# HGRN2 heads: the factor 1 - lb moves from the keys to the queries, both gates' sigmoids come first, and ScalarE copies the last level's score blocks

## Chip, core and metric

One NeuronCore of a Trainium2 chip runs the whole kernel. The metric is the device time of one execution in microseconds (us). The kernel before takes 2995.98 us (median of 3 runs, 2995.09 to 2998.92).

## The reference, cut to what matters

The network has two trunk layers: an HGRN2 gated linear recurrence in both directions, then a short convolution mixer, each followed by a dense SwiGLU FFN. All is float32. The change touches the recurrence alone. There are 8 heads of 128 channels, 1024 latent and 256 context tokens. For each head and direction:

```python
f = lb + (1.0 - lb) * jax.nn.sigmoid(zf)
log_f = jnp.log(jnp.maximum(f, F_FLOOR))
k = (1.0 - lb) * jax.nn.sigmoid(-zf)
...
o_inter = jnp.einsum("bhtk,bhkv->bhtv", qc * jnp.exp(cum), s)
scores = jnp.einsum("bhtk,bhsk,bhtsk->bhts", qc, kc, decay)
o = o_inter + jnp.einsum("bhts,bhsv->bhtv", scores, vc)
```

Every term of `o` holds q times k once, so the factor 1 - lb (one number for each channel) may stand on either.

## The kernel before

Each large product is three matmuls (high times high, high times low, low times high) of float32r halves. TensorE (PE) computes the projections of head h + 1 (five panels of 1024 x 128: both gates z_f and z_b, then q, v, g) and, between their pieces, the scan of head h. The first head (projections only) and the last (scan only) stand outside a loop of three passes with two heads each. All of it is written out by hand: each engine has its own program, and semaphores alone order them. On PE, `slots(n)` sets n pieces of three 512-column matmuls of the next head (or, behind a panel, a context block) between the steps of the scan.

The steps of one scan:

- ScalarE (ACT) computes the sigmoids of z_f and z_b into `gates` and of -z into `k`. VectorE (DVE) makes f of the gates, multiplies `k` by 1 - lb (L1726), applies the floor, then sums the keys of both directions (`k_sum`) and multiplies q by the gates into `q_all` (L1659).
- `diagonal`: PE multiplies q by k_sum for the diagonal of the scores (L782), and DVE takes it out of PSUM (`scores`, L1494).
- Seven levels, i = 0 to 6, each in two parts of four chunks. ACT merges the key halves into `k_both` (`merge_keys`), PE multiplies (`level`, L795), and DVE multiplies the keys (L1676) and queries (L1683) of both directions by the decay of their block, then copies the scores under a mask from PSUM (`copy_predicated`, L1685). After part 1 it multiplies the block totals (L1690).
- `key_transposes` and `key_values` (PE, L767 and L809), with ACT copying `k_tok` between them and DVE doing the states, forward first; then the outputs and their norm.

PSUM banks 4 and 5 take the scan's uses in turn, use 0, 2, ... and 1, 3, .... `scan_readers` names whose semaphore says that the bank's last use has been read. The forward key transposes come right behind level 6 in the same banks, and wait for the last totals_f too. ACT copies the next head's projections out of PSUM between its merges: z_f, z_b, then q (with the constant scale 128^-0.5) ahead of level 5 and between both parts of level 6. GpSimd (POOL) splits each weight panel into high and low parts (L522, L525).

Of the kernel before, what the change touches and what calls it, by code (L numbers as in the profile page):

```python
# [10 lines left out]
ALU = mybir.AluOpType  # L11
# [50 lines left out]
SCORE_EVACS = 16  # L62
# [54 lines left out]
def scan_readers(use):  # L117
    if use < U_DIAG:
        return [("scan_evac", ACT_EVACS, use)]
    if use < U_KF:  # L120
        return [("scores_evac", SCORE_EVACS, use - U_DIAG)]
    if use < U_KVF:
        return [("scan_evac", ACT_EVACS, 3 + use - U_KF)]
    if use < U_KB:
        return [("state_f", STATE_OPS, STATE_AT[use - U_KVF] - 1)]
    if use < U_KVB:
        return [("scan_evac", ACT_EVACS, 6 + use - U_KB)]
    if use < U_O:
# [23 lines left out]
def build_trunk(nc, x, ctx, cond, ada, ada_bias, norm_w, lb_raw, gnorm, conv_w,  # L152
# [105 lines left out]
    one_minus_lb = small("one_minus_lb", KB)  # L258
    gn = small("gn", 1)
# [19 lines left out]
    with ctx_mgr:  # L279
# [10 lines left out]
            sigmoids gates_done diag_ready scan_f scan_b k_merged scan_full scan_evac scores_evac state_f state_b  # L290
            gate_sig gs_ready o_squared o_gated o_sum_full ovar_done orstd_ready mix_ready mods_ready
# [6 lines left out]
        credit = {n: c for n, c in (("scan_evac", ACT_EVACS), ("scores_evac", SCORE_EVACS),  # L298
# [309 lines left out]
        def _(pe):  # L608
# [204 lines left out]
            def outputs(hh, part):  # L813

                pe.wait_ge(S["scores_evac"], hh * SCORE_EVACS + 2 * SCORE_EVACS)
                for d in (FWD, BWD):
                    pe.wait_ge(state_sem[d], hh * STATE_OPS + 2 * STATE_OPS)
                b = scan_use(hh, U_O + part)
                for c in range(4 * part, 4 * part + 4):
                    dst = bank(b, (c % 4) * P, (c % 4 + 1) * P)  # L820
                    pe.matmul(dst, v_tok[:, CCH + c, :], scores[:, c, :], start=True, stop=False)
                    pe.matmul(dst, state[FWD][:, c, :], chunk(qd[FWD], c), start=False, stop=False)
                    mm = pe.matmul(dst, state[BWD][:, c, :], chunk(qd[BWD], c), start=False, stop=True)
                mm.then_inc(S["scan_full"], 1)
# [294 lines left out]
        def _(act):  # L1119
# [46 lines left out]
            for name in ("scan_evac", "o_squared"):  # L1166
                act.sem_inc(S[name], credit[name])
# [50 lines left out]
            def head(gemm_of, scan_of, parity):  # L1218
# [26 lines left out]
                if hs is not None:  # L1245
# [5 lines left out]
                    act.wait_ge(S["scan_full"], hs * SCAN_USES + SCAN_USES)  # L1251
                    for d in (FWD, BWD):
                        copy(gates[d][:, :], z[d][:, :], "sigmoids", ACT.Sigmoid)
                        copy(k[d][:, :], z[d][:, :], "sigmoids", ACT.Sigmoid, scale=-1.0)
# [13 lines left out]
                def merge_keys(i, part):  # L1268

                    if i == 0:  # L1270

                        act.wait_ge(S["gates_done"], hs * 6 + 7)
# [38 lines left out]
                if hg is not None:  # L1311
# [4 lines left out]
                    evacuate(2, 0, cols(q, 0), scale=float(P) ** -0.5)  # L1316
# [3 lines left out]
                if hg is not None:  # L1320
                    evacuate(2, 1, cols(q, 1), scale=float(P) ** -0.5)
                if hs is not None:
                    merge_keys(6, 1)
                if hs is not None:
                    for part in range(3):
                        key_tokens(FWD, part)

                    for part in range(3):
                        key_tokens(BWD, part)
# [160 lines left out]
        def _(dve):  # L1490
# [27 lines left out]
            dve.wait_ge(S["params"], 7)  # L1518

# [130 lines left out]
            def head(gemm_of, scan_of):  # L1650
# [10 lines left out]
                def decay_level(i):  # L1661
# [3 lines left out]
                    for part in range(2):  # L1665
# [4 lines left out]
                        for d in (FWD, BWD):  # L1670
# [7 lines left out]
                            if d == BWD:  # L1678

                                dve.wait_ge(S["scores_evac"], hs * SCORE_EVACS + (SCORE_EVACS + 2 * i + part + 1))  # L1680
# [4 lines left out]
                        V.copy_predicated(scores[:, 4 * part:4 * part + 4, :],  # L1685
                                          masks[:, i, :].unsqueeze(1).broadcast_to([P, 4, P]),
                                          bank(use).rearrange("p (c t) -> p c t", t=P)
                                          ).then_inc(S["scores_evac"], 1)
                    for d in (FWD, BWD):
                        V.tensor_tensor(total_of(d, i + 1), tot[d][:, :, 0], tot[d][:, :, 1], ALU.mult  # L1690
                                        ).then_inc(scan_sem[d], 1)

# [24 lines left out]
                if hs is not None:  # L1717
                    lbs, oml = lb[:, bass.ds(hs, 1)], one_minus_lb[:, bass.ds(hs, 1)]
                    base_g = hs * 6 + 1
# [51 lines left out]
                elif hg is not None:  # L1771
                    for a in range(ADA_GROUP):
# [206 lines left out]
```

## Time and profile before

| | us |
|---|---|
| median of 3 runs | 2995.98 |
| the profiled execution, its own time | 2991.44 |
| its span | 2989.4 |
| PE busy | 2810.2 (94%) |
| DVE busy | 1446.8 (48%) |
| ACT busy | 721.7 (24%) |
| POOL busy | 761.7 (25%) |

An engine that is idle costs nothing unless the chain of work that ends last runs through it. The seven scans that share PE with projections lie between 130 and 892 us of the span, the scan of the last head between 892 and 1000 us. Granted clock is TensorE's, 1.00 for 2.4 GHz and 0.50 for 1.2 GHz. In rows of a timeline the first number is the start, the second the time to the end of the group, both in us, and the bracket tells how long the engine stood idle before, and what released it.

### The profile page before, as it was taken

To read this page: it belongs to the slowest core of one execution; us is meant where nothing else is said; L and a number is where in the kernel's file an instruction comes from. 1 tells how busy PE (TensorE), PEld (TensorE's weight loads), DVE (VectorE), ACT (ScalarE), POOL (GpSimd) and SP (SyncE) were. 2 spreads that over 40 slices of the span, in tenths; PEclk is the share of its full clock that TensorE was granted. 3 is DMA by queue.
4 is the path that set the end of the run, shared out by engine and by line. 5 is a ranking of instruction groups with operands and counts; after the bars stand their busy time and mean duration, and the time that the engine had idled before them with its cause. 6 is when DMAs were issued, how large, how long until landed. Compare 5 with 4: busy or idle time off the path is not lost.

```text
span 2989.4 us, 36417 instructions
## 1 busy us (share of the span) xinstructions
PE 2810.2 (94%) x13776; PEld 2358.3 (79%) x13776; DVE 1446.8 (48%) x2083; ACT 721.7 (24%) x1251; POOL 761.7 (25%) x361
## 2 busy tenths in 40 slices
PE   7989999999986899999999998999899999999997
PEld 5778778777875688888888887888688888888886
DVE  6377576577658232343242346556732323332236
ACT  5223223223323251111111116111143111111112
POOL 3322121212114311222222231344702222222222
PEclk9999999999997999999999999999999999999999
DMA  5111111111110201121111110332201111111111
GB/s 227 64 36 49 45 41 52 36 57 36 36 36 28 99 15 51 49 78 63 63 62 58 63 64 22 127 112 98 91 15 36 49 44 48 49 49 49 49 49 71
DMA packets 48742, 176.89 MB, mean 59 GB/s; under 512 B 5872, under 2 KB 5872, under 8 KB 48624
## 3 DMA queue, kind: packets, MB, share of 16 engines
q1 hardware_dynamic: 48624, 175.24, 17.2%
q8 instruction: 83, 1.36, 0.2%
q14 instruction: 35, 0.29, 0.0%
HBM read 171.02 MB, written 4.19 MB: 59 GB/s over the span
## 4 chain that ended last, share of the span: by engine, by line
PE 80%; DVE 12%; ACT 3%; issue 2%; DMA 1%; SPq 0%; POOL 0%; DVEq 0%; ACTq 0%; POOLq 0%
PE psum L613 18%; PE psum L615 17%; PE psum L614 17%; PE psum L1011 4%; PE psum L1012 4%; PE psum L1013 4%; PE psum L795 3%; DVE q_all L1683 2%; DVE k_all L1676 2%; PE psum L659 2%; PE psum L845 2%; PE psum L846 2%; PE psum L847 2%; DVE h_lo L1494 1%; DVE scores L1685 1%
## 5 line engine op out<-in xcount | busy, mean ns | idle before, releaser
L613 PE MATMUL psum<-h_hi,w_hi 128*128 128x512 f32 x2336 | 938.0, 402 | 8.0 <-POOL w_lo L525 4.9
L615 PE MATMUL psum<-h_hi,w_lo 128*128 128x512 f32 x2336 | 913.3, 391 | 0.0
L614 PE MATMUL psum<-h_lo,w_hi 128*128 128x512 f32 x2336 | 912.6, 391 | 0.0
L568 POOL TENSOR_TENSOR w_lo<-w_raw,w_hi 128x1024 fp32r<-128x1024 f32 x116 | 280.0, 2414 | 1032.6 <-ACT w_hi L1121 1032.6
L615 PEld LDWEIGHTS psum<-h_hi,w_lo 128*128 128x128 f32 x2336 | 440.1, 188 | 94.1
L613 PEld LDWEIGHTS psum<-h_hi,w_hi 128*128 128x128 f32 x2336 | 441.3, 189 | 90.7 <-POOL w_lo L525 5.3
L614 PEld LDWEIGHTS psum<-h_lo,w_hi 128*128 128x128 f32 x2336 | 441.6, 189 | 81.0
L522 POOL TENSOR_TENSOR w_hi<-w_raw,zero 128x1024 fp32r<-128x1024 f32 x74 | 151.7, 2050 | 1041.9 <-PE psum L613 926.8
L1494 DVE TENSOR_TENSOR hidden<-gate_act,up_copy 128x512 f32<-128x512 f32 x88 | 75.8, 861 | 655.3 <-ACT up_copy L1121 655.3
L1494 DVE TENSOR_TENSOR y<-y,psum 128x512 f32<-128x512 f32 x288 | 194.8, 686 | 202.4 <-PE psum L1013 199.9
L1011 PE MATMUL psum<-w_hi,hidden_hi 128*128 128x512 f32 x640 | 250.0, 391 | 0.3 <-DVE y L1494 0.3
L1013 PE MATMUL psum<-w_hi,hidden_lo 128*128 128x512 f32 x640 | 249.5, 390 | 0.0
L1012 PE MATMUL psum<-w_lo,hidden_hi 128*128 128x512 f32 x640 | 249.5, 390 | 0.0
L1121 ACT ACTIVATE w_hi<-w_raw 128x1024 fp32r<-128x1024 f32 x116 | 122.4, 1055 | 351.0 <-PE psum L613 178.9
L795 PE MATMUL psum<-q_all,k_both 128*128 128x128 f32 x896 | 138.8, 302 | 59.5 <-ACT k_both L1121 18.0
L795 PEld LDWEIGHTS psum<-q_all,k_both 128*128 128x128 f32 x896 | 127.5, 204 | 83.3 <-issue 24.4
L525 POOL TENSOR_TENSOR w_lo<-w_raw,w_hi 128x1024 fp32r<-128x1024 f32 x74 | 191.0, 2581 | 5.8
L1641 DVE SCALAR_TENSOR_TENSOR ada_acc<-ada_raw,silu_cond,ada_acc 128x512 f32<-128x512 f32 x140 | 158.8, 1134 | 51.5 <-DMA ada_raw<-in_ada 47.2
L1121 ACT ACTIVATE gate_act<-psum 128x512 f32<-128x512 f32 x88 | 52.6, 598 | 380.1 <-PE psum L615 380.1
L1121 ACT ACTIVATE up_copy<-psum 128x512 f32<-128x512 f32 x88 | 52.6, 598 | 377.9 <-PE psum L615 377.9
L1011 PEld LDWEIGHTS psum<-w_hi,hidden_hi 128*128 128x128 f32 x640 | 120.3, 188 | 25.6 <-DVE y L1494 0.9
L1013 PEld LDWEIGHTS psum<-w_hi,hidden_lo 128*128 128x128 f32 x640 | 120.4, 188 | 25.2
(216 smaller groups left out, 3537.0 us busy)
## 6 DMA issues: line engine op xcount, KB each, us to landing
w_raw<-in_w_ffn_in SPq DMA_DIRECT2D x88, 512.0 KB, 3.5
ada_raw<-in_ada SPq DMA_DIRECT2D x80, 512.0 KB, 4.4
w_raw<-in_w_ffn_out SPq DMA_DIRECT2D x44, 512.0 KB, 3.5
w_raw<-in_w_hgrn_in SPq DMA_DIRECT2D x40, 512.0 KB, 5.9
w_raw<-in_w_conv_in SPq DMA_DIRECT2D x24, 512.0 KB, 4.9
ada_first<-in_ada SPq DMA_DIRECT2D x4, 2048.0 KB, 15.5
x_start<-in_x SPq DMA_DIRECT2D x4, 1024.0 KB, 18.7
w_raw<-in_w_hgrn_out SPq DMA_DIRECT2D x8, 512.0 KB, 3.6
```

The costliest lines, as they stand in the source:

```text
L525: pool.tensor_tensor(lo[:, :], w_raw[:, slot, :], hi[:, :], ALU.subtract).then_inc(S["panel_split"], 1)
L568: pool.tensor_tensor(lo[:, :], w_raw[:, slot, :], hi[:, :], ALU.subtract).then_inc(S["panel_split"], 1)
L613: begin = pe.matmul(out_ap, hi[:, a:b], rhs_hi, start=first, stop=False)
L614: pe.matmul(out_ap, hi[:, a:b], rhs_lo, start=False, stop=False)
L615: return begin, pe.matmul(out_ap, lo[:, a:b], rhs_hi, start=False, stop=last)
L795: mm = pe.matmul(bank(b, (c % 4) * P, (c % 4 + 1) * P), chunk(k_both, c), both(q_all, c * P, 1 << i), start=True, stop=True)
L1011: begin = pe.matmul(dst, hidden_hi[buf][:, kb, tokens], hi[:, cols], start=first, stop=False)
L1012: pe.matmul(dst, hidden_hi[buf][:, kb, tokens], lo[:, cols], start=False, stop=False)
L1013: return begin, pe.matmul(dst, hidden_lo[buf][:, kb, tokens], hi[:, cols], start=False, stop=last)
L1121: nc.scalar.activation(dst, src, func, **kw).then_inc(S[sem], 1)
L1494: V.tensor_tensor(dst, a, b, op).then_inc(S[sem], 1)
L1641: V.scalar_tensor_tensor(ada_acc[:, :], src, weight, ada_acc[:, :], ALU.mult, ALU.add).then_inc(S["ada_step"], 1)
```

## The change

The keys are no longer multiplied: a copy of `one_minus_lb` times 128^-0.5 is made once (`q_scale`), DVE copies the next head's column of it to `head_scale`, and ACT takes that as the scale operand when it copies q out of PSUM. ACT does the sigmoids in the order gates_f, gates_b, k_f, k_b. At level 6 the mask holds just one 64 x 64 block for each direction and chunk, and ACT copies these blocks in place of DVE's masked copy of all 512 columns.

```diff
-SCORE_EVACS = 16
+SCORE_EVACS = 14
+
+LAST = LEVELS - 1
...
+    if use < U_LEVEL + 2 * LAST:
+        return [("scores_evac", SCORE_EVACS, use - U_DIAG)]
     if use < U_KF:
-        return [("scores_evac", SCORE_EVACS, use - U_DIAG)]
+        return [("last_scores", 4, 2 * (use - U_LEVEL - 2 * LAST) + 1)]
...
                 pe.wait_ge(S["scores_evac"], hh * SCORE_EVACS + 2 * SCORE_EVACS)
+                pe.wait_ge(S["last_scores"], hh * 4 + (credit["last_scores"] + 4))
...
                     for d in (FWD, BWD):
                         copy(gates[d][:, :], z[d][:, :], "sigmoids", ACT.Sigmoid)
+                    for d in (FWD, BWD):
                         copy(k[d][:, :], z[d][:, :], "sigmoids", ACT.Sigmoid, scale=-1.0)
...
-                    evacuate(2, 0, cols(q, 0), scale=float(P) ** -0.5)
+                    act.wait_ge(S["head_scaled"], hg + 1)
+                    evacuate(2, 0, cols(q, 0), scale=head_scale[:, 0:1])
...
-                    evacuate(2, 1, cols(q, 1), scale=float(P) ** -0.5)
+                    evacuate(2, 1, cols(q, 1), scale=head_scale[:, 0:1])
                 if hs is not None:
                     merge_keys(6, 1)
                 if hs is not None:
+                    b = 1 << LAST
+                    for part in range(2):
+                        src = bank(scan_bank(U_LEVEL + 2 * LAST + part)).rearrange("p (c t) -> p c t", t=P)
+                        for d in (FWD, BWD):
+                            rows, cs = slice(K_HALF[d] * b, K_HALF[d] * b + b), slice(Q_HALF[d] * b, Q_HALF[d] * b + b)
+                            copy(scores[rows, 4 * part:4 * part + 4, cs], src[rows, :, cs], "last_scores")
                     for part in range(3):
                         key_tokens(FWD, part)
...
+            V.tensor_scalar(q_scale[:, :], one_minus_lb[:, :], float(P) ** -0.5, None, ALU.mult
+                            ).then_inc(S["params"], 1)
...
-                        V.copy_predicated(scores[:, 4 * part:4 * part + 4, :],
-                                          masks[:, i, :].unsqueeze(1).broadcast_to([P, 4, P]),
-                                          bank(use).rearrange("p (c t) -> p c t", t=P)
-                                          ).then_inc(S["scores_evac"], 1)
+                        if i < LAST:
+                            V.copy_predicated(scores[:, 4 * part:4 * part + 4, :],
+                                              masks[:, i, :].unsqueeze(1).broadcast_to([P, 4, P]),
+                                              bank(use).rearrange("p (c t) -> p c t", t=P)
+                                              ).then_inc(S["scores_evac"], 1)
...
+                def scale_of_head():
+
+                    V.tensor_copy(head_scale[:, :], q_scale[:, bass.ds(hg, 1)]).then_inc(S["head_scaled"], 1)
...
                     for d in (FWD, BWD):
-                        dve.wait_ge(S["sigmoids"], hs * 4 + (2 * d + 1))
+                        dve.wait_ge(S["sigmoids"], hs * 4 + (d + 1))
                         V.tensor_scalar(gates[d][:, :], gates[d][:, :], oml, lbs, ALU.mult, ALU.add
                                         ).then_inc(S["gates_done"], 1)
-                        dve.wait_ge(S["sigmoids"], hs * 4 + (2 * d + 2))
-                        V.tensor_scalar(k[d][:, :], k[d][:, :], oml, None, ALU.mult).then_inc(S["gates_done"], 1)
-                        dve.wait_ge(S["gates_done"], base_g + (3 * d + 1))
+                        dve.wait_ge(S["gates_done"], hs * 4 + (2 * d + 2))
                         V.tensor_scalar(gates[d][:, :], gates[d][:, :], F_FLOOR, None, ALU.max
                                         ).then_inc(S["gates_done"], 1)
-                    dve.wait_ge(S["gates_done"], base_g + 6)
+                    dve.wait_ge(S["sigmoids"], hs * 4 + 4)
+                    if hg is not None:
+                        scale_of_head()
+                    dve.wait_ge(S["gates_done"], hs * 4 + 5)
                     tt(k_sum[:, :], lat(k[FWD]), lat(k[BWD]), ALU.add, "diag_ready")
```

VectorE at the head's start, before the change (k_all holds k of both directions):

```order
L1723 TENSOR_SCALAR gates_f<-gates_f,one_minus_lb,lb 128x1280
L1725 REGISTER_ALU
L1726 TENSOR_SCALAR k_all<-k_all,one_minus_lb 128x1280
L1727 ISA
L1728 TENSOR_SCALAR gates_f<-gates_f 128x1280
L1722 REGISTER_ALU
L1723 TENSOR_SCALAR gates_b<-gates_b,one_minus_lb,lb 128x1280
L1725 REGISTER_ALU
L1726 TENSOR_SCALAR k_all<-k_all,one_minus_lb 128x1280
L1727 REGISTER_ALU
L1728 TENSOR_SCALAR gates_b<-gates_b 128x1280
```

The same place after it:

```order
L1745 TENSOR_SCALAR gates_f<-gates_f,one_minus_lb,lb 128x1280
L1747 REGISTER_ALU
L1748 TENSOR_SCALAR gates_f<-gates_f 128x1280
L1745 TENSOR_SCALAR gates_b<-gates_b,one_minus_lb,lb 128x1280
L1747 REGISTER_ALU
L1748 TENSOR_SCALAR gates_b<-gates_b 128x1280
L1715 ISA
L1715 COPY head_scale<-q_scale 128x1
L1753 REGISTER_ALU
L1510 TENSOR_TENSOR k_sum<-k_all 128x1024
```

Both multiplications of k_all are gone from ahead of k_sum, and a copy of one column has come in.

VectorE at level 6, part 1, and the totals behind it, before the change:

```order
L1676 TENSOR_TENSOR k_all<-k_all,totals_even_f 128x4x64
L1683 TENSOR_TENSOR q_all<-q_all,totals_even_f 128x4x64
L1676 TENSOR_TENSOR k_all<-k_all,totals_even_b 128x4x64
L1680 REGISTER_ALU
L1683 TENSOR_TENSOR q_all<-q_all,totals_even_b 128x4x64
L1685 COPY_PREDICATED scores<-masks,psum 128x512
L1690 TENSOR_TENSOR totals_f<-totals_even_f 128x10
```

The same place after it:

```order
L1694 TENSOR_TENSOR k_all<-k_all,totals_even_f 128x4x64
L1702 TENSOR_TENSOR q_all<-q_all,totals_even_f 128x4x64
L1694 TENSOR_TENSOR k_all<-k_all,totals_even_b 128x4x64
L1698 REGISTER_ALU
L1702 TENSOR_TENSOR q_all<-q_all,totals_even_b 128x4x64
L1710 TENSOR_TENSOR totals_f<-totals_even_f 128x10
```

The totals, for which the forward key transposes wait, follow the queries at once.

ScalarE from the second half of q to the first tokens of the keys, after the change (before it the four rows of scores are not there, and q has no operand head_scale):

```order
L1128 ACTIVATE q<-psum,head_scale 128x512
L1285 REGISTER_ALU
L1288 REGISTER_ALU
L1128 ACTIVATE k_both<-k_all 128x4x64 x2
L1241 REGISTER_ALU
L1128 ACTIVATE scores<-psum 64x4x64 x2
L1241 REGISTER_ALU
L1128 ACTIVATE scores<-psum 64x4x64 x2
L1241 REGISTER_ALU
L1128 ACTIVATE k_tok<-psum 128x512
```

The four block copies stand behind the last merge of level 6 and ahead of the first k_tok.

## Rows read from the trace of the kernel before

**Rows 1.** The page, chain that ended last: share of the span by engine

```profile
PE 80%; DVE 12%; ACT 3%; issue 2%; DMA 1%; SPq 0%; POOL 0%; DVEq 0%; ACTq 0%; POOLq 0%
```

**Rows 2.** Windows, PE: us, busy (instructions), granted clock, DMA share, GB/s

```profile
588.01:695.94 107.93, 99.49 (x593) 0.98 0.13 45
695.94:802.17 106.23, 98.03 (x592) 1.00 0.13 45
```

**Rows 3.** Waits of PE from 150 to 890 us: total, times, longest

```profile
PE psum L795 <- ACT k_both L1121: 18.0, 12, 1.5
...
PE psum L767 <- DVE totals_f L1690: 14.3, 7, 2.1
```

**Rows 4.** Timeline of PE, scan of head 2

```profile
369.33 1.56 PE L795 MATMUL psum<-q_all,k_both 128*128 128x128 f32 x8 [1.51 <-ACT k_both L1121]
...
406.33 1.59 PE L795 MATMUL psum<-q_all,k_both 128*128 128x128 f32 x8 [2.09 <-DVE k_all L1676]
...
417.17 1.13 PE L795 MATMUL psum<-q_all,k_both 128*128 128x128 f32 x8 [1.48 <-ACT k_both L1121]
...
424.46 0.65 PE L767 MATMUL psum<-ident,k_all 128*128 128x128 f32 x4 [2.05 <-DVE totals_f L1690]
```

**Rows 5.** Timeline of DVE, level 6 of head 2

```profile
418.33 0.42 DVE L1676 TENSOR_TENSOR k_all<-k_all,totals_even_f 128x256 f32<-128x256 f32 x1 [1.57 <-PE psum L795]
...
423.57 0.71 DVE L1685 COPY_PREDICATED scores<-masks,psum 128x512 f32<-128x512 uint8 x1
424.18 0.15 DVE L1690 TENSOR_TENSOR totals_f<-totals_even_f 128x10 f32<-128x10 f32 x1
```

**Rows 6.** Timeline of ACT, the same stretch

```profile
415.72 0.60 ACT L1121 ACTIVATE q<-psum 128x512 f32<-128x512 f32 x1 [5.85 <-PE psum L615]
...
425.15 0.60 ACT L1121 ACTIVATE k_tok<-psum 128x512 f32<-128x512 f32 x1 [8.22 <-PE psum L767]
```

**Rows 7.** Groups of DVE from 130 to 1000 us: busy us, mean ns

```profile
L1685 DVE COPY_PREDICATED scores<-masks,psum 128x512 f32<-128x512 uint8 x112 | 81.1, 724 | 0.0
...
L1726 DVE TENSOR_SCALAR k_all<-k_all,one_minus_lb 128x1280 f32<-128x1280 f32 x16 | 18.3, 1143 | 0.0
```

**Rows 8.** Timelines of ACT and DVE, start of head 2

```profile
368.35 1.38 ACT L1121 ACTIVATE k_both<-k_all 128x256 f32<-128x256 f32 x4
...
364.17 1.22 DVE L1659 TENSOR_TENSOR q_all<-q,gates_f 128x1024 f32<-128x1024 f32 x1
...
371.03 0.56 DVE L1676 TENSOR_TENSOR k_all<-k_all,gates_f 128x384 f32<-128x384 f32 x1 [2.17 <-PE psum L795]
```

**Rows 9.** Groups of ACT over the span, forms apart

```profile
L1121 ACT ACTIVATE mod_start<-psum,mods,in_scale 128x256 f32<-128x256 f32 x16 | 8.1, 557 | 2.3 <-PE psum L659 2.3
...
L1121 ACT ACTIVATE z_f<-psum 128x256 f32<-128x256 f32 x8 | 3.1, 382 | 31.2 <-PE psum L615 31.2
```

**Rows 10.** Timelines of DVE, ACT and PE, start of the last head

```profile
901.50 2.30 DVE L1659 TENSOR_TENSOR q_all<-q,gates_f 128x1024 f32<-128x1024 f32 x1
...
907.87 1.40 ACT L1121 ACTIVATE k_both<-k_all 128x256 f32<-128x256 f32 x4
...
908.88 1.44 PE L795 MATMUL psum<-q_all,k_both 128*128 128x128 f32 x5 [3.52 <-DVE scores L1494]
```

**Rows 11.** Timelines of DVE and PE, level 6 of the last head

```profile
961.55 0.71 DVE L1685 COPY_PREDICATED scores<-masks,psum 128x512 f32<-128x512 uint8 x1
962.16 0.41 DVE L1676 TENSOR_TENSOR k_all<-k_all,totals_even_f 128x256 f32<-128x256 f32 x1
...
964.32 2.28 PE L767 MATMUL psum<-ident,k_all 128*128 128x128 f32 x9 [3.38 <-DVE totals_f L1690]
```

**Rows 12.** Windows, PE, columns as in rows 2

```profile
188.39:191.80 3.41, 3.41 (x12) 0.50 0.75 286
...
406.84:410.25 3.41, 3.41 (x12) 0.50 0.91 346
...
625.29:628.70 3.41, 3.41 (x13) 0.50 0.89 321
...
734.52:737.93 3.41, 3.41 (x21) 1.00 0.63 229
```

More of the change, by code:

```diff
@@ L258, in build_trunk @@
     one_minus_lb = small("one_minus_lb", KB)
+    q_scale = small("q_scale", KB)
+    head_scale = small("head_scale", 1)
     gn = small("gn", 1)
@@ L289, in build_trunk @@
             proj_full proj_evac y_scaled x_updated row_full row_ready
-            sigmoids gates_done diag_ready scan_f scan_b k_merged scan_full scan_evac scores_evac state_f state_b
-            gate_sig gs_ready o_squared o_gated o_sum_full ovar_done orstd_ready mix_ready mods_ready
+            sigmoids gates_done diag_ready scan_f scan_b k_merged scan_full scan_evac scores_evac last_scores state_f state_b
+            gate_sig head_scaled gs_ready o_squared o_gated o_sum_full ovar_done orstd_ready mix_ready mods_ready
             mix_hi mix_split
@@ L297, in build_trunk @@
         state_sem = [S["state_f"], S["state_b"]]
-        credit = {n: c for n, c in (("scan_evac", ACT_EVACS), ("scores_evac", SCORE_EVACS),
+        credit = {n: c for n, c in (("scan_evac", ACT_EVACS), ("scores_evac", SCORE_EVACS), ("last_scores", 4),
                                     ("state_f", STATE_OPS), ("state_b", STATE_OPS), ("o_squared", 2),
@@ L1165, in _ @@
             act.sem_inc(S["ctx_evac"], 1)
-            for name in ("scan_evac", "o_squared"):
+            for name in ("scan_evac", "last_scores", "o_squared"):
                 act.sem_inc(S[name], credit[name])
@@ L1270, in merge_keys @@
                     if i == 0:
-                        act.wait_ge(S["gates_done"], hs * 6 + 7)
+                        act.wait_ge(S["gates_done"], hs * 4 + 5)
                         act.wait_ge(S["scan_full"], hs * SCAN_USES + (SCAN_USES + U_DIAG + 2))
@@ L1678, in decay_level @@
                             if d == BWD:
-                                dve.wait_ge(S["scores_evac"], hs * SCORE_EVACS + (SCORE_EVACS + 2 * i + part + 1))
+                                dve.wait_ge(S["scores_evac"], hs * SCORE_EVACS
+                                            + (SCORE_EVACS + min(2 * i + part + 1, SCORE_EVACS)))
                             n0, n1 = (CTX + q0) // (2 * b), (CTX + q1) // (2 * b)
@@ L1718, in head @@
                     lbs, oml = lb[:, bass.ds(hs, 1)], one_minus_lb[:, bass.ds(hs, 1)]
-                    base_g = hs * 6 + 1
                     for d in (FWD, BWD):
-                        dve.wait_ge(S["sigmoids"], hs * 4 + (2 * d + 1))
+                        dve.wait_ge(S["sigmoids"], hs * 4 + (d + 1))
                         V.tensor_scalar(gates[d][:, :], gates[d][:, :], oml, lbs, ALU.mult, ALU.add
                                         ).then_inc(S["gates_done"], 1)
-                        dve.wait_ge(S["sigmoids"], hs * 4 + (2 * d + 2))
-                        V.tensor_scalar(k[d][:, :], k[d][:, :], oml, None, ALU.mult).then_inc(S["gates_done"], 1)
-                        dve.wait_ge(S["gates_done"], base_g + (3 * d + 1))
+                        dve.wait_ge(S["gates_done"], hs * 4 + (2 * d + 2))
                         V.tensor_scalar(gates[d][:, :], gates[d][:, :], F_FLOOR, None, ALU.max
                                         ).then_inc(S["gates_done"], 1)
-                    dve.wait_ge(S["gates_done"], base_g + 6)
+                    dve.wait_ge(S["sigmoids"], hs * 4 + 4)
+                    if hg is not None:
+                        scale_of_head()
+                    dve.wait_ge(S["gates_done"], hs * 4 + 5)
                     tt(k_sum[:, :], lat(k[FWD]), lat(k[BWD]), ALU.add, "diag_ready")
@@ L1771, in head @@
                 elif hg is not None:
+                    scale_of_head()
                     for a in range(ADA_GROUP):
```

## The prediction, made before the run

> **What bounds the kernel now.** I read the chain that ended last first [rows 1]: 80% of it is PE and 12% DVE, so only what makes PE wait counts, and DVE's own work where it stands between PE's. The windows by head come next [rows 2]: the two heads shown, which share PE with projections, take 107.9 and 106.2 us, 99.5 and 98.0 of them PE busy. What is to be had is the 8 us that PE stands idle, and the list of PE's waits says where [rows 3]: 18.0 us behind ACT's k_both in 12 waits of at most 1.5, and 14.3 us behind DVE's totals_f in 7, which is 2.04 in each head. The timeline puts them in place [rows 4]: 1.51 us ahead of level 0, 2.09 ahead of level 5, 1.48 ahead of part 1 of level 6, and 2.05 ahead of the forward key transposes. The seven scans that share PE repeat this nearly to the hundredth. The last head has no projections to fill with, and there DVE is on the path for most of the levels.
>
> **The masked copy of level 6, the overlapped heads.** The transposes at 424.46 wait for totals_f, and on DVE totals_f stands right behind the masked copy: 423.57 to 424.18 [rows 4, 5]. Its pitch of 0.61 us comes off that wait, and leaves 1.44 of 2.05. The copy of part 0 gives nothing: DVE stands idle 1.57 us ahead of part 1's first multiplication, waiting for PE [rows 5]. So 7 heads x 0.61 = 4.3 us. For this ACT's block copies must be early enough. ACT has nothing to do for 8.22 us up to its first k_tok at 425.15 [rows 6]. Part 0's scores have been ready since before that, part 1's since about 418.3, when DVE began on that part [rows 5]. No row shows a 64 x 4 x 64 copy. From below it costs nothing, from above a PSUM copy of 256 columns takes 0.38 [rows 9] and one of 512 0.60 [rows 6]; I take 0.38. Four are 1.5 us, the last ends near 420, some 3.8 us before the transposes can start. They are hidden. If that cover went, a pair would cost PE at most 0.8 (1.2 by the upper end).
>
> **The scale operand of q.** Ahead of part 1 of level 6 ACT is on the path: it copies q at 415.72, then merges two keys, and PE starts at 417.17 [rows 4, 6]. A copy with a scale operand in SBUF instead of a constant: mod_start, which has two such operands (scale and bias), takes 557 ns, and z_f of the same size without any 382 [rows 9]. Half the difference is 0.09 us; it may be 0 or 0.175. 7 x 0.09 = +0.6 us. The first half of q is not on the path.
>
> **The keys' multiplications and the sigmoids' order.** The two multiplications take 18.3 us of DVE in 16 instructions, with POOL's splits stretching some of them [rows 7]. In the overlapped heads DVE is done with all of its first stage and then idle 2.17 us before level 0's result arrives at 371.03, and the wait of PE before it is ended by ACT's merges at 368.35, which follow a copy of z_f that waits for PE itself [rows 4, 8]. Being earlier there moves nothing; at most 0.1 us, where k_sum comes just in time for the diagonal. The copy of head_scale (one column) stands in that slack too. I take 0.1 for all seven, 0 to 0.7.
>
> **The last head.** At its start PE waits 3.52 us for level 0 until 908.88, by the list for DVE's scores. But ACT's merges begin at 907.87, the four taking 1.40, so the first two are done near 908.6 [rows 10]: with DVE earlier, 0.2 us is what this wait can give. More can come sideways. The first product of q takes 2.30 us there against 1.22 elsewhere [rows 8, 10], because POOL is at work beside it on h_lo; with two multiplications gone, DVE does part of this before POOL starts, POOL gets through its long queue sooner, and DVE's slow stretch ends sooner. Below: 0.2. Above: both multiplications at their mean of 1.14, so 2.3 [rows 7]. Nearer to the lower end, since PE and ACT hold the start: 0.9. At level 6 DVE runs without a gap from the masked copy at 961.55 to the keys at 962.16, and PE waits 3.38 us for totals_f [rows 11]. So both copies count there: 2 x 0.61 = 1.2 us.
>
> **Direct sum.** -4.3 + 0.6 - 0.1 - 0.9 - 1.2 = -5.9 us.
>
> **The clock.** In the overlapped heads the granted clock drops to 0.50 (1.2 GHz) seven times, for 3.41 us each: in five heads behind the wait of 2.09 at level 5, and in two behind the wait at level 0; the stretch at 406.84 is one [rows 12]. Its price is 1.70 us: head 4 has one and takes 107.93, head 5 has none and takes 106.23, with as many matmuls [rows 2]. Head 5 waits at level 5 as long, within 0.2 us, and keeps 1.00 [rows 12]. So it isn't the wait's length alone, but where in time it falls. The drops behind level 5 stand 218.45 us apart for two heads (188.39 and 406.84) and again 218.45 (406.84 and 625.29) [rows 12]: the heads, in this kernel, keep step with whatever sets these moments. Heads that are each 0.5 us shorter (0.61 less 0.09) fall out of step, and the drops should spread over the places by chance. Seven of the 14 places (level 0 and level 5, seven heads) have one now. I take five after: -2 x 1.70 = -3.4 us. Ends: two left (-8.5), or nine (+3.4).
>
> [...] By the Trainium skill (TensorE: Matmul & The Clock Gate, HAM oscillation) idle gaps as short as these should not lower the clock; then the term is 0 and the sum -5.9. The trace disagrees: it drops seven times behind gaps of 1.5 to 2.1 us. The same page (The HAM clock gate) also says that the number of slow matmuls changes from run to run of one kernel, by where it starts, which no row of one execution can show; by it each timed run would have its own number of drops.
>
> **Total.** -5.9 - 3.4 = -9.3 us on 2991.44, the profiled execution's own time, is 2982.1. The median of the runs lies 4.5 us above that execution, and I carry the difference over: 2995.98 - 9.3 = 2986.7 us. Within 0.2% (6.0 us) a measurement of this kernel can't tell it from no change, so the line is at 2990.0.
>
> **Rivals.**
> - Forecast, 0.58: direct sum and fewer drops, 2981 to 2990, most likely 2986.7.
> - Only the direct part, with as many drops as before or up to two more, 0.28: 2990.1 to 2993.5. For it: the place of a drop is not mine to compute, and -5.9 by itself is just short of the line. It is also what the page's rule of thumb gives, at 2990.1. Against it: seven drops come of a coincidence of periods that the change ends.
> - All of what is taken from DVE counts, 0.10: 18.3 us of key multiplications and 7 x 0.61 more for part 0's copies on top, or nearly all drops gone: below 2981, down to 2965. Against it the idle 2.17 and 1.57 us of DVE [rows 5, 8].
> - Slower, 0.04: ACT's block copies become the last thing for which the key transposes wait. They stand in order behind the merges of level 6 and in front of k_tok, and everything behind them (six k_tok, then v_t) is late with them. To cost 6 us against before, that is 12 with the gains, each of 8 heads must lose 1.5: part 1's pair would have to end at 425.3 and not 419.9, 3.5 us a copy where the nearest rows have 0.38 and 0.60 [rows 6, 9].
>
> **Range and chances.** The lower end is all drops but two gone and the upper bound in the last head, 2995.98 - 8.5 - 5.9 - 1.4 = 2980 (I take 2979.5); the upper is the direct sum less the 0.7 of the lower bound there, with one or two drops more, near 2993. Faster by over 0.2%: the forecast and the large gain, 0.68. Within 0.2%: 0.28. Slower: 0.04.
>
> **What would show it.** Right: PE's wait for the first forward key transposes near 1.4 us (2.05 now) and still ended by DVE's totals; ACT's copies over by about 420 on that clock; q's copy near 0.69; the waits at level 0 and 5 as long as now; the last head's level-6 wait shorter by 1.2; five stretches at 0.50 or so between 150 and 890 us, no longer 218.45 apart. Wrong: a key transpose that waits for ACT's scores, block copies over 1 us, seven or more drops, or DVE waiting less than before at level 0 with PE's wait there shorter too, which would mean that the first stage was on the path after all.

## The result, and the profile after

Six timed executions of the changed kernel have a median of 2982.04 us (2981.3 to 2988.69); six of the kernel before 2998.9 (2995.09 to 3004.35). The ratio is 0.9948, 95% interval 0.9937 to 0.9959: faster by half a per cent, inside the range forecast and 4.7 us under the predicted number. The drop, 16.9 us, is larger than the 9.3 forecast: of the difference, 2.9 us is the kernel before, which came out that much above the 2995.98 from which the forecast was counted. A second series (e10 below) gave a drop of 9.6. The profiled execution took 2981.93 us with a span of 2979.9, against 2991.44 and 2989.4 before: 9.5 us less.

The page, the chain that ended last by engine, answers to [rows 1]:

```profile
PE 82%; DVE 11%; ACT 3%; issue 3%; DMA 1%; POOL 0%; DVEq 0%; SPq 0%; ACTq 0%; POOLq 0%
```

The waits of PE from 150 to 885 us, after (total, times, longest), answer to [rows 3]:

```profile
PE psum L801 <- ACT k_both L1128: 17.1, 11, 1.7
PE psum L801 <- DVE k_all L1694: 14.9, 12, 2.1
PE psum L773 <- DVE totals_f L1710: 10.1, 7, 1.5
```

The seven waits for totals_f have gone from 14.3 to 10.1 us: 4.2, where 4.3 was forecast. PE's timeline of head 2 after, against [rows 4], shows the same four places:

```profile
363.73 1.56 PE L801 MATMUL psum<-q_all,k_both 128*128 128x128 f32 x8 [1.50 <-ACT k_both L1128]
...
400.73 1.72 PE L801 MATMUL psum<-q_all,k_both 128*128 128x128 f32 x8 [2.03 <-DVE k_all L1694]
...
411.75 1.13 PE L801 MATMUL psum<-q_all,k_both 128*128 128x128 f32 x8 [1.66 <-ACT k_both L1128]
...
418.44 0.65 PE L773 MATMUL psum<-ident,k_all 128*128 128x128 f32 x4 [1.46 <-DVE totals_f L1710]
```

The waits at level 0 and level 5 stay as they were. The wait behind the copy of q is longer (1.48 before; 1.66 in heads 0 and 2, 1.57 in the four other heads looked at), and the last is 1.46 in place of 2.05. ACT beside it, against [rows 6]:

```profile
410.12 0.69 ACT L1128 ACTIVATE q<-psum,head_scale 128x512 f32<-128x512 f32 x1 [5.74 <-PE psum L621]
410.71 0.71 ACT L1128 ACTIVATE k_both<-k_all 128x256 f32<-128x256 f32 x2
411.32 0.77 ACT L1128 ACTIVATE scores<-psum 64x256 f32<-64x256 f32 x2
412.91 0.78 ACT L1128 ACTIVATE scores<-psum 64x256 f32<-64x256 f32 x2 [0.83 <-PE psum L801]
419.13 0.60 ACT L1128 ACTIVATE k_tok<-psum 128x512 f32<-128x512 f32 x1 [5.44 <-PE psum L773]
```

The four block copies fill part of the gap that was 8.22 us, are over at 413.7, and ACT then stands idle for 5.44 us: they delay nobody. Their price over the whole span, by form, and that of q beside it (busy us, mean ns):

```profile
L1128 ACT ACTIVATE scores<-psum 64x256 f32<-64x256 f32 x32 | 12.0, 375 | 7.5 <-PE psum L801 7.1
L1128 ACT ACTIVATE q<-psum,head_scale 128x512 f32<-128x512 f32 x16 | 11.0, 688 | 77.4 <-PE psum L621 77.4
```

DVE at level 6 of the same head, after, against [rows 5]:

```profile
412.91 0.43 DVE L1694 TENSOR_TENSOR k_all<-k_all,totals_even_f 128x256 f32<-128x256 f32 x1 [2.39 <-PE psum L801]
413.26 2.12 DVE L1702 TENSOR_TENSOR q_all<-q_all,totals_even_f 128x256 f32<-128x256 f32 x1
415.30 2.60 DVE L1694 TENSOR_TENSOR k_all<-k_all,totals_even_b 128x256 f32<-128x256 f32 x1
417.82 0.41 DVE L1702 TENSOR_TENSOR q_all<-q_all,totals_even_b 128x256 f32<-128x256 f32 x1
418.16 0.15 DVE L1710 TENSOR_TENSOR totals_f<-totals_even_f 128x10 f32<-128x10 f32 x1
```

The masked copy is gone from ahead of totals_f. What now fills the path is two multiplications of 2.12 and 2.60 us between two of about 0.42 with as many elements, and POOL, in the same stretch, is at its split of a weight panel:

```profile
413.19 1.90 POOL L528 TENSOR_TENSOR w_hi<-w_raw,zero 128x1024 fp32r<-128x1024 f32 x1 [19.65 <-PE psum L619]
415.17 2.44 POOL L531 TENSOR_TENSOR w_lo<-w_raw,w_hi 128x1024 fp32r<-128x1024 f32 x1
```

DVE's two slow multiplications and POOL's two instructions run together, start and end within 0.3 us. So 3.9 us of the stretch before totals_f (2.12 and 2.60 less twice 0.42) stand beside POOL's work, and the change left that as it was.

At the start of a head DVE has lost its two key multiplications, and idles 3.18 us where it idled 2.17 [rows 8], while PE's wait of 1.50 there is what it was:

```profile
365.43 0.56 DVE L1694 TENSOR_TENSOR k_all<-k_all,gates_f 128x384 f32<-128x384 f32 x1 [3.18 <-PE psum L801]
```

One place ahead of it did move, by too little for the list of waits. PE's diagonal needs k_sum. Before, at the start of head 3 (DVE, then PE):

```profile
470.94 1.23 DVE L1494 TENSOR_TENSOR k_sum<-k_all 128x1024 f32<-128x1024 f32 x1
471.90 0.39 PE L615 MATMUL psum<-h_hi,w_lo 128*128 128x512 f32 x1
472.30 1.15 PE L782 MATMUL psum<-q,k_sum 128*128 128x128 f32 x8
```

After:

```profile
463.59 1.22 DVE L1510 TENSOR_TENSOR k_sum<-k_all 128x1024 f32<-128x1024 f32 x1
465.92 0.39 PE L621 MATMUL psum<-h_hi,w_lo 128*128 128x512 f32 x1
466.14 1.05 PE L788 MATMUL psum<-q,k_sum 128*128 128x128 f32 x8
```

Before, k_sum ended at 472.17 and the diagonal began behind it, 0.40 us after the start of the matmul ahead; after, k_sum ends at 464.81 and the diagonal follows by 0.22. From the key transposes of one head to level 0 of the next this makes the interval shorter by 0.08 to 0.27 us, 1.25 in all six.

**The last head.** PE's timeline after, its start and its level 6, answers to [rows 10, 11]:

```profile
901.21 2.05 PE L801 MATMUL psum<-q_all,k_both 128*128 128x128 f32 x8 [4.75 <-ACT k_both L1128]
...
955.22 1.10 PE L773 MATMUL psum<-ident,k_all 128*128 128x128 f32 x8 [1.60 <-DVE totals_f L1710]
```

and ACT's, ahead of the first:

```profile
893.09 7.38 ACT L1128 ACTIVATE h_hi<-mix 128x512 fp32r<-128x512 f32 x14
900.37 1.38 ACT L1128 ACTIVATE k_both<-k_all 128x256 f32<-128x256 f32 x4
```

The first level waits for ACT, whose four merges stand behind 14 copies for h_hi. DVE's head start of 2 us buys little there. At level 6 the wait fell from 3.38 to 1.60.

**The clock.** Between 150 and 890 us seven stretches stand at 0.50 again, of 3.41 us each; two of them (PE; columns as in [rows 2]):

```profile
401.09:404.50 3.41, 3.41 (x13) 0.50 0.93 341
...
619.54:622.95 3.41, 3.41 (x14) 0.50 0.61 244
```

The others begin at 186.05, 291.86, 472.77, 510.31 and 725.35. Six of the seven come with the wait at level 5 or right behind it, one behind level 0.

**Where the 9.5 us went**, by the starts of level 0 in head 0, head 6 and the last head (before 150.47, 802.17 and 908.88 us; after 147.73, 795.29 and 901.21): 2.7 lie ahead of head 0. Of these, 2.0 are in one group of 40 matmuls on the stream, at line L665 now, that took 4.80 us where it had taken 6.83, at half clock; e7, which has the whole change, takes 6.90 there, so this comes of where a stretch falls and not of the change. Another 0.4 is a shorter wait for a weight panel, and 0.3 is at the diagonal of head 0, the only part that belongs to the change. From head 0 to head 6 it is 651.70 less 647.56, 4.1 us; from there to the last head 106.71 less 105.92, 0.8; to the key transposes of the last head 55.44 less 54.01, 1.4; behind them 0.4. So in these two traces, each with seven half-clock stretches, 6.6 to 7.0 us are the change's own, against a direct sum of 5.9. The stretches whose saving made the other 3.4 of the forecast are not missing from this trace.

### The profile page after: what moved, and what is told of

It reads as the page before. It is cut to its first block, busy times and chain, and to the rows that moved or that the text cites. A ratio compares the mean times of both kernels' runs of the same rounds, so it can differ in the third digit from the quotient of the medians.

```text
span 2979.9 us, 36433 instructions
## 1 busy us (share of the span) xinstructions
PE 2809.6 (94%) x13776; PEld 2358.0 (79%) x13776; DVE 1424.9 (48%) x2060; ACT 733.9 (25%) x1283; POOL 761.1 (26%) x361
## 4 chain that ended last, share of the span: by engine, by line
PE 82%; DVE 11%; ACT 3%; issue 3%; DMA 1%; POOL 0%; DVEq 0%; SPq 0%; ACTq 0%; POOLq 0%
PE psum L619 18%; PE psum L621 17%; PE psum L620 17%; PE psum L1018 4%; PE psum L1020 4%; PE psum L1019 4%; PE psum L801 3%; DVE q_all L1702 2%; DVE k_all L1694 2%; PE psum L852 2%; PE psum L853 2%; PE psum L854 2%; PE psum L665 2%; DVE h_lo L1510 1%; PE psum L815 1%
```

## The experiments

**e1: the kernel before, unchanged.** What one kernel does from one execution to the next had to be known first.

> The kernel before, unchanged, to see how far its executions differ and why. My theory: what differs is how many stretches at half clock an execution has (1.70 us each), which depends on where the waits fall and not on the kernel's text. Then a longer execution has a lower mean clock, about 0.0006 less for each stretch, its waits are the same to 0.1 us, and the ratio is 1.000 within 0.002. Rival: the spread comes from DMA or from the start, and the mean clock doesn't follow the time.

Measured: ratio 0.9994 (0.9984 to 1.0005), with 11 executions from 2990.28 to 3003.91 us. Its profiled execution took 2991.53 us and has the same seven half-clock stretches as the one of [rows 12], each 0.1 us earlier, so again with steps of 218.45:

```profile
188.29:191.70 3.41, 3.41 (x13) 0.50 0.83 327
406.74:410.15 3.41, 3.41 (x12) 0.50 0.85 327
```

The other ten executions lie from 1.3 us below it to 12 us above. The longer ones have the lower mean clock (0.974 for the longest), as expected; how many stretches each of them had is not shown, since only one was traced.

**e2: the block copies alone**; keys are multiplied, the sigmoids' order and q's constant are as before.

```diff
-                    evacuate(2, 0, cols(q, 0), scale=head_scale[:, 0:1])
+                    evacuate(2, 0, cols(q, 0), scale=float(P) ** -0.5)
...
+                        V.tensor_scalar(k[d][:, :], k[d][:, :], oml, None, ALU.mult).then_inc(S["gates_done"], 1)
```

> The block copies alone; keys multiplied as before, q with the constant scale, sigmoids in the old order. My theory (the copies bring nearly all): wait for totals_f 1.44 in place of 2.05 in seven heads, 1.2 us less in the last head's levels, q's copy 0.60 and the wait behind it 1.48; -5.5 us direct, and with it whatever the clock gives, so a ratio near 0.996. Rival (the key multiplications on the path in every head make up the part of the result that exceeds the forecast): -5.5 us and no more, 0.998.

Measured: 2987.62 us (five), ratio 0.996 (0.9947 to 0.9973), as expected. As far as these timings tell, this part alone gives the gain:

```profile
PE psum L773 <- DVE totals_f L1708: 10.1, 7, 1.5
```

**e3: the factor alone**; q carries 1 - lb and the sigmoids are in their new order, DVE makes the masked copy of level 6 as before.

```diff
-                        if i < LAST:
+                        if i < LEVELS:
                             V.copy_predicated(
```

> The factor on q, the sigmoids' order and the scale operand alone; level 6 copied by DVE under the mask as before. My theory: the wait for totals_f stays 2.05, the one behind q grows by 0.09 (0.6 us in all), the last head gains 0.2 to 2.3: -0.3 us direct, ratio 0.998 to 1.001. Rival: the 18.3 us of key multiplications count in every head: -10 us or more, 0.997 or less, with a shorter wait at level 0.

Measured: 3000.35 us (twelve), ratio 1.0003 (0.9993 to 1.0013): nothing that the timings can tell, with 18.3 us of DVE work gone. Its mean clock, 0.9750, lies under that of the kernel before beside it, 0.9761, so a gain of about 1 us may hide in this. PE's wait for totals_f is what it was before:

```profile
PE psum L771 <- DVE totals_f L1701: 14.3, 7, 2.1
```

Its profiled execution, at 3003.93 us, had 14 half-clock stretches between 148 and 745 us, the first and the last of them

```profile
149.67:153.08 3.41, 3.41 (x18) 0.50 0.00 0
740.18:743.59 3.41, 3.41 (x14) 0.50 0.94 371
```

**e4: the changed kernel with a constant as q's scale**, and ACT doesn't wait for head_scale. Its output lacks the factor 1 - lb, which is 1 here, since the reference has one HGRN layer.

```diff
-                    evacuate(2, 1, cols(q, 1), scale=head_scale[:, 0:1])
+                    evacuate(2, 1, cols(q, 1), scale=float(P) ** -0.5)
```

> The changed kernel, but ACT copies q with the constant scale again and doesn't wait for head_scale (with one HGRN layer the reference's lb is 0, so the values are the same). My theory: q's copy 0.60 in place of about 0.69, the wait behind it 0.09 shorter in seven heads: 0.6 us less than the changed kernel, within what the clock scatters, ratio 0.994 to 0.996. Rival (the operand is free, its cost hidden): no difference in that wait.

Measured: 2985.95 us (five), ratio 0.9956 (0.9943 to 0.9969). The wait behind q is back to 1.48 in four heads of seven (1.51, 1.57 and 1.34 in the others); 0.6 us over seven heads is less than these timings can tell.

**e5: the forward and backward key transposes wait for their direction's keys**, not for the totals. What they read is complete with the keys of part 1; for the forward ones that was at 413.3 in the changed kernel's head 2, while PE waited until 418.44.

```diff
                 if part == 0:
-                    pe.wait_ge(scan_sem[d], hh * SCAN_STEPS + SCAN_STEPS)
+                    pe.wait_ge(scan_sem[d], hh * SCAN_STEPS + (1 + 5 * LAST + 3))
```

> The changed kernel, and the key transposes wait only until the keys of level 6, part 1, are multiplied, no longer for the queries and totals behind them. My theory (what is left of that wait is DVE's rest of the level, and everything behind it follows PE): 1.45 us less in each of seven heads, over 1 us in the last: -11 us against the changed kernel, ratio to before 0.990 to 0.992, no wait left there. Rival: the wait goes on to the banks, held by ACT's score copies, or to the states; then a wait of about the same length stands at the second or third transposes or at the products of keys and values.

Measured: 2973.36 us (four, 2972.28 to 2975.12), ratio 0.9906 (0.9889 to 0.9924). As expected, the wait is gone from the overlapped heads: PE's transposes of head 2 have no bracket, while DVE still works beside POOL (PE, then DVE):

```profile
415.85 0.60 PE L773 MATMUL psum<-ident,k_all 128*128 128x128 f32 x4
```

```profile
412.27 2.12 DVE L1702 TENSOR_TENSOR q_all<-q_all,totals_even_f 128x256 f32<-128x256 f32 x1
414.31 2.61 DVE L1694 TENSOR_TENSOR k_all<-k_all,totals_even_b 128x256 f32<-128x256 f32 x1
```

**e6: the same early wait in the kernel before.** There DVE's masked copy still holds the PSUM bank that the transposes want.

> The same edit on the kernel before. There the second group of forward transposes needs the bank that DVE's masked copy of part 1 still reads. My theory: the first transposes don't wait, the second wait about 0.8 us, so 1.2 of 2.05 us go in each of seven heads, -8.5 us direct; it shows that the block copies by ACT are worth another 0.8 us a head once DVE isn't waited for. Ratio 0.996 to 0.998. Rival (the masked copy costs nothing but its own 0.61 us): no wait at the second transposes and 2.05 us gone.

Measured: 2983.29 us (four), ratio 0.9943 (0.9924 to 0.9962), more than expected: 16 us less by means where 8.5 were reckoned, of which the mean clock (0.9778 against 0.9757) makes some 6. The waits of PE from 150 to 885 us:

```profile
PE psum L767 <- DVE scores L1685: 5.6, 7, 0.8
```

So the old masked copy has a second price that the prediction did not see: with the totals out of the way it costs 0.8 us a head as the bank's last reader. The block copies by ACT take both away. Of the 10 us by which e5 is faster than e6, these waits are 5.6; the earlier diagonals and the start of the last head (1.6 and 0.3 us, below) make up to 1.9 more, and the rest was not followed.

**e7: DVE's first two `ada_rows` moved** from between levels 3 and 4 to behind level 6, in the changed kernel. They were the rows ahead of the wait at level 5.

```diff
                         decay_level(i)
-                        if hg is not None and i == 3:
-                            for a in range(2):
-                                ada_rows(hg, a)
+                    if hg is not None:
+                        for a in range(2):
+                            ada_rows(hg, a)
                     for d in (FWD, BWD):
```

> The changed kernel with the first four ada_rows instructions of a head moved from between levels 3 and 4 to between level 6 and the states, where DVE is idle over 4 us. My theory on the clock (the wait of 2.1 us at level 5 is what brings most of the stretches at half clock): that wait falls under 0.3 us, no more than one or two stretches are left behind level 5, mean clock of the executions 0.982 or more; 14 us of waits and some 8 us of clock less, ratio to before 0.986 to 0.989. Rival (the stretches have another cause): the waits go, the mean clock stays at 0.978 to 0.980, and the ratio is 0.990. Second rival: the loads of ada panels are held up, and with them a weight panel; then POOL waits for a load and PE for POOL.

Measured: 2959.22 us (four, 2954.89 to 2961.17), ratio 0.9856 (0.9837 to 0.9876), a little better than expected. The waits of PE from 150 to 885 us:

```profile
PE psum L801 <- ACT k_both L1128: 22.3, 17, 1.6
...
PE psum L801 <- DVE k_all L1694: 2.6, 6, 0.4
```

The wait at level 5 is gone; part of it has turned into one for ACT. And the wait for totals_f is gone from the overlapped heads as well, without e5's edit. POOL's split now falls behind DVE's level 6, and the multiplication that took 2.12 takes 0.42 (DVE, then POOL, of head 2):

```profile
404.80 0.42 DVE L1702 TENSOR_TENSOR q_all<-q_all,totals_even_f 128x256 f32<-128x256 f32 x1
```

```profile
415.91 1.89 POOL L528 TENSOR_TENSOR w_hi<-w_raw,zero 128x1024 fp32r<-128x1024 f32 x1 [27.99 <-DMA w_raw<-in_w_hgrn_in]
```

Counted from level 0 of head 2, DVE's level 6 comes 2.8 us earlier than in the changed kernel and POOL's split 8.3 us later: POOL now waits for the load of its panel, and nobody waits for POOL. SyncE issues its loads in order, and that of the panel stands behind two of `ada_raw`, which wait until DVE has done its `ada_rows`. In the changed kernel these two went out at 396.76, in e7, which does the rows later:

```profile
407.40 1.91 SPq L388 DMA_DIRECT2D ada_raw<-in_ada  x2
409.50 11.27 SPq L382 DMA_DIRECT2D w_raw<-in_w_hgrn_in  x3
```

So the second rival's first half came true, and here it helped. Only two half-clock stretches are left (at 150.64 and 550.00); the mean clock of the four executions is 0.9805, between the 0.982 expected and the first rival's 0.980.

**e8: e5 and e7 together.**

> Both edits together on the changed kernel. If they are independent the savings add: 33 us against the changed kernel at most, ratio to before 0.982 to 0.986, with both waits under 0.3 us. If the moved ada_rows delay the totals that the first states need, a new wait of up to 1.5 us stands at the forward states or at the second key-value products.

Measured: 2958.73 us (four), ratio 0.986 (0.9843 to 0.9878). The two gains do not add, and the ratio is the upper end of what was expected: e7 had already taken away the wait that e5 removes.

**e9: e8, with ACT's merges ahead of its copies of the next head's projections** at level 0, level 5 and level 6, where a merge had to wait until PE had finished a projection.

```diff
-                    for half in range(2):
-                        evacuate(0, half, cols(z[FWD], half, CTX))
-                merge_level(0)
+                    evacuate(0, 0, cols(z[FWD], 0, CTX))
+                if hs is not None:
+                    merge_keys(0, 0)
+                if hg is not None and hs is not None:
+                    evacuate(0, 1, cols(z[FWD], 1, CTX))
+                if hs is not None:
+                    merge_keys(0, 1)
...
+                if hs is not None:
+                    merge_keys(5, 0)
...
                     evacuate(2, 0, cols(q, 0), scale=head_scale[:, 0:1])
-                merge_level(5)
+                if hs is not None:
+                    merge_keys(5, 1)
...
-                if hg is not None:
-                    evacuate(2, 1, cols(q, 1), scale=head_scale[:, 0:1])
                 if hs is not None:
                     merge_keys(6, 1)
+                if hg is not None:
+                    evacuate(2, 1, cols(q, 1), scale=head_scale[:, 0:1])
```

> The version with both edits, and ACT merges the keys of level 0 part 0, level 5 part 0 and level 6 part 1 ahead of the copies of z_f and q that it did first. My theory (those copies wait for PE's own projections, so PE waits for itself): the waits behind k_both of 1.5, 0.9 and 1.57 us in a head fall under 0.4 in all, about 25 us less in seven heads, no stretch at half clock is left between 150 and 850 us, mean clock 0.982 or more; against that version's 2958.7 this gives 2930 to 2936 us, ratio to before 0.977 to 0.980. Rival: ACT's later copies hold up PSUM banks or DVE's chain ends later than PE arrives, so that most of the wait stays under another name: 2945 or more.

Measured: 2923.98 us (four, 2920.24 to 2926.55), ratio 0.9753 (0.9734 to 0.9771), better than expected. The waits of PE from 150 to 885 us:

```profile
PE psum L801 <- ACT k_both L1128: 1.8, 5, 0.4
```

That list had 23.8 us in e8, in the same window. By means e9 is 35.0 us faster than e8: 22.0 from this list, some 7 from the clock (0.9825 against 0.9802, at 3 us for 0.001, as worked out under e10); the other 6 were not followed. One half-clock stretch is left, at 532.78, where none was expected. This version beats both kernels, by 2.5% and 2.1%.

**e10: the changed kernel, unchanged.** The first six executions had five within 1.5 us of each other and one 6 us above.

> The changed kernel, unchanged, to see how firm its six executions are. If fewer stretches at half clock are what the change brings beyond its direct part, the mean clock of these executions is again near 0.979 and above that of the kernel before beside them (0.975 to 0.977), and the ratio is 0.994 to 0.996. Rival (the first six were lucky): mean clock 0.977, ratio 0.997 to 0.998, which is the direct part alone.

Measured: 2987.04 us (eleven, 2980.53 to 2991.47), ratio 0.997 (0.9958 to 0.9981) to a before of 2996.68. That is the ratio which the expectation gave to its rival, that the first six were lucky; the mean clock, 0.9776, lies between the 0.979 of the theory and the rival's 0.977, and above the 0.9764 of the kernel before beside it. Its profiled execution has six stretches.

The mean clock recorded for each execution ties these together. Over the 57 executions of the kernel before for which it is on record, in three series on two chips, the mean time is 2997.7 us at a mean clock of 0.9762; the fastest is 2989.04 at 0.979, the slowest 3007.52 at 0.973. Over 17 of the changed kernel it is 2985.3 at 0.9782. Time and clock go together within each kernel (correlation -0.90 and -0.94; 2.9 and 2.1 us for 0.001). One stretch of 3.41 us at half speed is 0.0006 of the mean clock and costs 1.7 us, so 3.0 us for 0.001: time at half clock accounts for most of the scatter of 18 us. The difference of the means, 12.4 us, is then 0.0020 of clock, 6.0 us, and 6.4 for the rest. In e10's series alone, against the kernel before beside it, it is 9.9 us: 0.0011 of clock, 3.3 us, and 6.6 for the rest. Both times the rest is near the direct part as the two traces gave it (6.6 to 7.0). But the mean clock is that of the whole span: outside the overlapped heads the trace of before holds 104.5 us at half clock, that of after 97.3 and that of e10 108.1. Where the timed executions of the changed kernel have less of it is not shown.

## Why the prediction came true, step by step

- **The masked copy in the overlapped heads, -4.3 us: right.** -4.2 by the list of waits, in the changed kernel and in e2 alike, still ended by totals_f. In e3, without it, the list stays at 14.3.
- **The block copies hidden: right.** 375 ns each, within 1% of the 0.38 taken. They end at 413.7, 4.7 us before the transposes start, where 3.8 was reckoned.
- **q's scale operand, +0.6: right.** 688 ns against 598, and the wait behind it longer by 0.09 in most heads, by 0.18 in two (in e10 by 0.09 there too), 0.6 to 0.8 us in all; e4 takes most of it back. In the timed runs it is below what can be told.
- **The keys' multiplications, -0.1: the place was right, the size was not.** DVE's idle time grew by 1.0 us a head and PE's wait at level 0 did not move, as forecast. But at the diagonal, where the prediction allowed 0.1 us in all and 0.7 at most, k_sum had come late in every head: 0.3 us in head 0 and 1.25 from there to head 6, so 1.6. e3 shows it too (52.53 us from the key transposes of head 2 to level 0 of head 3, where before and e2 have 52.79). The rival "all of what is taken from DVE counts" falls even so: with the last head it is some 2 us of 18.3.
- **The last head's start, -0.9: too large.** ACT holds it, behind its copies for h_hi. From the key transposes of head 6 to level 0 of the last head before, e1 and e2 take 53.81 us, and after, e10, e3 and e4, which have the factor, 53.52 or 53.53: 0.3, near the lower bound of 0.2. Nothing came sideways by way of POOL either: e3, which has this part alone, takes 56.05 from there to its key transposes, where before takes 55.44.
- **The last head's level 6, -1.2: right within what two traces of one kernel differ.** The interval from its level 0 to the key transposes is 1.4 us shorter and the wait 1.8 in the changed kernel's first trace, 0.4 and 1.3 in e10's, with a different share at half clock.
- **The clock, -3.4: the sign held on the mean, the reason is not borne out, and so the number is luck.** The price of a stretch was right. The mean clock rose, by 3.3 us' worth in e10's series and by 6.0 in both series together, where 3.4 was forecast; that it rose by fewer stretches in the overlapped heads is not shown. The term was argued from one trace: the heads keep step with whatever sets the moments, and shorter heads would fall out of step. The prediction itself named seven or more drops as a sign that this is wrong. The changed kernel's trace has seven again, and those behind level 5 come once a head in six heads running, 105.8 or 109.2 us apart; before had them once a head in five heads, each 109.2 us after the last (188.39, 297.61, 406.84, 516.07, 625.29, of which the prediction names every second one). So they followed the shorter heads and did not fall out of step. In e10 there are six, at partly other places. The starting point was off too: the profiled execution of before, with seven, was among the fastest (clock 0.979, where the mean is 0.9762), and e1's profiled one is its double. If the number of stretches has a spread over the executions of one kernel, as the mean clocks suggest, no count in one trace shows it. In e2 to e4 the profiled executions, with 5, 14 and 8 stretches, lie from 2981.54 to 3003.93, and with 1.7 us taken off for each, from head 0 to head 6, they come to 636.7, 638.1 and 634.8 us, where before has 639.8 and after 635.6. (e3's is 1.7 below before, where its own terms give 0.7, so this correction is good to about 1 us.)

The rival "only the direct part" gave 2990.1 to 2993.5, and the median of the longer series (2987.04) lies 3 us below it. It is not excluded by that series alone: the direct sum on 2995.98 is a ratio of 0.998, and e10's interval reaches 0.9981. Only with the first six executions taken in is the gain clearly more than the direct part's. The sum of the direct terms was good to about a microsecond (5.9 against 6.6 to 7.0), in part by luck: the keys' term was too small by 1.5 us and that of the last head's start too large by 0.6.

**Open.** Why the changed kernel has the higher mean clock is not shown. In the overlapped heads most of the stretches came in or right behind PE's waits of 1.5 to 2.1 us. The wait that the change shortened, 2.05 us for totals_f, is not among these: in before, e1 and e3, which have it in seven heads each, none of the 28 stretches stands behind it, and e5, where it is gone entirely, had nine and a mean clock of 0.9778, no better than the changed kernel. The waits at level 5, which e5 leaves and e7 removes, look like the ones that matter: e7 and e8 have two stretches each, e9, which has lost the waits of 1.5 for k_both too, has one. No run had the waits at level 5 alone removed with that for totals_f kept.

## What to carry to other kernels

Find for each stall which of several waits ends last, and what that instruction really needs: one number in a semaphore wait (e5) gave as much as the change, and that with a few lines of order on the two helping engines (e9) five times as much, with no work removed. A busy sum is no price: 18.3 us of DVE work came off for some 2 us, 4.3 us at the right place came off in full. A list of waits has a threshold: a stall of 0.2 us in every head did not show in it, and only intervals between fixed points of two traces did show it. Where an effect is under 0.5%, one profile and a handful of runs can mislead by as much as the effect; put the mean clock of each execution beside its time and compare at equal clock.

## What was not expected of the hardware

- One kernel, unchanged, scatters by 18 us, and the mean clock follows the time (correlation -0.90). In the overlapped heads TensorE runs at 1.2 GHz in stretches of 3.41 us: 5 to 14 of them in the traces of before, after and e2 to e4, most of them in or right behind a wait of PE of 1.5 to 2.1 us. So a stall can cost more than its length: e7 took 19.2 us off the lists of waits (level 5, scores and totals_f, less what ACT's grew) and 26.7 off the mean time.
- By the rule of thumb in the Trainium skill (TensorE: Matmul & The Clock Gate, HAM oscillation) gaps this short should leave the clock alone; every trace of this study disagrees, with one to 14 drops in the overlapped heads. The same page (The HAM clock gate) says that the number of slow matmuls varies from run to run of one kernel. The mean clocks of the 57 executions of before, 0.973 to 0.979, fit that; the two traces of it have the same seven stretches.
- POOL's split of a weight panel stretches a DVE multiplication of two SBUF operands from 0.42 to 2.12 and 2.60 us, and these end 0.3 us behind POOL's instructions. Where POOL's split fell beside level 6, it set one of PE's waits in each of seven heads.
